# Keys, receptance and output projection of a recurrent block in three reduced-precision passes, and half of the values ahead of the triangular matrices

## The reference

```
h = rms_norm(x, norm_g)
dx = jnp.pad(h, ((0, 0), (1, 0), (0, 0)))[:, :-1] - h
xr, xw, xk, xv, xa, xg = (h + dx * mu[i] for i in range(6))
r = xr @ w_r
...
k = xk @ w_k
v = xv @ w_v
...
o = wkv7_scan(rh, decay, kh, vh, -kk, kk * ah)
...
y = (o + bonus.reshape(Bn, Sn, Dn)) * g.astype(f32)
return y.astype(x.dtype) @ w_o, v_first
```

## Time and profile before

| | us |
|---|---|
| median of 3 runs | 976.53 (975.99 to 976.78) |
| the profiled execution | 981.15 |
| its span | 979.4 |
| PE busy | 955.4 (98%) |
| DVE busy | 668.4 (68%) |
| ACT busy | 442.1 (45%) |
| one middle group, from second-rank matmuls to second-rank matmuls (91.47 to 156.51) | 65.04 |

### The profile page before, as it was taken

The page is one execution under the profiler, slowest core; times in us unless marked ns, Lnnn a source line. Parts: engine busy times, 40 slices in busy tenths (PEclk is TensorE's granted clock), DMA queues, the critical chain, the costliest instruction groups (busy, mean ns, idle before and its releaser), DMA issues.

```text
span 979.4 us, 17605 instructions
## 1 busy us (share of the span) xinstructions
PE 955.4 (98%) x6716; PEld 826.2 (84%) x6716; DVE 668.4 (68%) x1269; ACT 442.1 (45%) x708; POOL 84.5 (9%) x66
## 2 busy tenths in 40 slices
PE   8999999999999999999998999999999999999998
PEld 6778688686788888888897999999999798888887
DVE  7863755647647666666696878888887666666665
ACT  3313214114225444444355566666656554444442
POOL 0211000000010000000021222121212000000000
PEclk9999999999989999999998999999999999999999
DMA  9310320500513766666468455445543147666661
GB/s 303 135 57 1 115 72 1 172 14 4 171 43 99 224 192 193 188 189 194 115 215 240 116 157 154 131 128 162 148 143 116 46 131 221 190 190 188 185 188 59
DMA packets 195126, 136.85 MB, mean 140 GB/s; under 512 B 7278, under 2 KB 185966, under 8 KB 194940
## 3 DMA queue, kind: packets, MB, share of 16 engines
q1 hardware_dynamic: 195068, 136.03, 47.2%
HBM read 134.96 MB, written 1.05 MB: 139 GB/s over the span
## 4 chain that ended last, share of the span: by engine, by line
PE 63%; issue 24%; DVE 6%; POOL 4%; ACT 2%; POOLq 0%; DVEq 0%
PE wide L446 34%; PE bank L446 28%; POOL gsm L1834 4%; DVE work L1309 2%; DVE work L1312 1%; ACT work L994 1%; DVE x L1309 1%; DVE wsp L1309 0%; ACT L994 0%; DVE work L1567 0%; PE bank L469 0%; DVE am L1309 0%; DVE work L1399 0%; POOL small L1834 0%; DVE work L1619 0%
## 5 line engine op out<-in xcount | busy, mean ns | idle before, releaser
L446 PE MATMUL bank<-wpj,hkq 128*128 128x384 f32 x1152 | 216.9, 342 | 2.6 <-ACT Vs L994 1.8
L446 PEld LDWEIGHTS bank<-wpj,hkq 128*128 128x128 f32 x1152 | 199.9, 190 | 6.6 <-ACT wpj L994 2.8
L446 PE MATMUL wide<-hsp,wsp 128*128 128x256 f32 (+2 forms) x1120 | 193.4, 329 | 0.0
L446 PEld LDWEIGHTS wide<-hsp,wsp 128*128 128x128 f32 x1120 | 172.4, 190 | 23.0 <-DVE hsp L1309 0.6
L1309 DVE TENSOR_TENSOR wsp<-ring,wsp 128x1024 fp32r<-128x1024 f32 (+1 forms) x88 | 150.7, 1752 | 4.2 <-ACT wsp L994 4.2
L994 ACT ACTIVATE wsp<-ring 128x1024 fp32r<-128x1024 f32 (+1 forms) x88 | 130.3, 1485 | 21.9 <-PE wide L446 13.3
L1309 DVE TENSOR_TENSOR wpj<-ring,wpj 128x1536 fp32r<-128x1536 f32 x48 | 84.2, 1754 | 23.0 <-ACT wpj L994 23.0
L446 PE MATMUL bank<-wsp,asp 128*128 128x512 f32 x396 | 98.1, 392 | 0.0
L1834 POOL TENSOR_TENSOR gsm<-gsm,mhalf 128x6 f32<-128x6 f32 (+1 forms) x40 | 62.4, 1593 | 312.8 <-DVE gsm L1757 215.1
L446 PEld LDWEIGHTS bank<-wsp,asp 128*128 128x128 f32 x396 | 71.7, 189 | 13.1
L994 ACT ACTIVATE wpj<-ring 128x1536 fp32r<-128x1536 f32 x48 | 71.2, 1484 | 24.3 <-PE bank L446 16.6
(11 more groups left out here) (243 smaller groups left out, 1136.9 us busy)
## 6 DMA issues: line engine op xcount, KB each, us to landing
ring<-in_f_w_gu SPq DMA_DIRECT2D x88, 512.0 KB, 5.9
ring<-in_w_kv SPq DMA_DIRECT2D x96, 256.0 KB, 3.5
ring<-in_f_w_down SPq DMA_DIRECT2D x44, 512.0 KB, 3.7
ring<-in_b_w_q SPq DMA_DIRECT2D x48, 256.0 KB, 3.5
wmix<-in_a_w_k SPq DMA_DIRECT2D x4, 1024.0 KB, 7.8
wmix<-in_a_w_r SPq DMA_DIRECT2D x4, 1024.0 KB, 10.0
wmix<-in_a_w_v SPq DMA_DIRECT2D x4, 1024.0 KB, 5.2
wmix<-in_a_w_o SPq DMA_DIRECT2D x4, 1024.0 KB, 5.6
```

Of the source, the lines that this page charges most:

```text
L446: return pe.matmul(o, a, b, start=start, stop=stop)
```

## The change

Three projections of groups 1 to 3 go to the three-pass form: receptance (`project_parts` on `rw_hi`, `xr_hi`, `xr_lo`), keys, and the output product inside the loop (`product_o` for `it < NGRP`). Group 0's receptance and keys, the values, and the output product behind the last group stay float32. New copies: ACT writes `x_hi` (two tensors of 2048 columns, in group 0), `kw_hi`, `rw_hi`, `ow_hi` (2048 columns, in groups 0 to 2, for the group after) and `y_hi` (512 columns, in groups 1 to 3). DVE writes the low parts, in pieces of 1024 columns.

Four further moves: the value quarter that stood behind the second matrices now stands ahead of `turn_norms` (groups 1 to 3); the four scans of DVE run while POOL takes the root (`norm_output(it, 1, scans)`); a one-element sigmoid at a group's end brings the sigmoid table in ahead of the square; and several tiles share memory to make room. On SP the feed-forward loads wait once more, for the last receptance.

```
@@ DVE, in the levels and behind them
+                    if not behind and l in (1, 2):
+                        dve.wait_ge(S("act_x_hi"), 1)
+                        dve.wait_ge(S("pe_k"), 1)
+                        low_half("xk", l - 1)
+                    kw = l - (1 if behind else 3)
+                    if ahead and kw in (0, 1):
+                        low_key_weights(kw)
...
+                if not behind:
+                    dve.wait_ge(S("act_x_hi"), 2)
+                    dve.wait_ge(S("pe_r"), 1)
+                    low_half("xr", 0)
+                    low_half("xr", 1)
+                if ahead:
+                    low_query_weights()
+                if ahead and behind:
+                    low_output_weights()
                 dve.wait_ge(S("pe_S"), it + 1)
...
-                norm_output(it + 1, 0)
+                norm_output(it + 1, 0, None if behind else low_output_weights)
@@ ACT, behind the copies of the matrices and at the group's end
+                if ahead:
+                    act.wait_ge(s_wm[1], it * 16 + 32)
+                    A(kw_hi, wmix[:, 1, :], ACT.Copy).then_inc(S("act_mix_hi"), 1)
                 act.wait_ge(S("pe_v"), it + 1)
                 A(vT, bank[6], ACT.Copy).then_inc(S("act_v"), 1)
...
                 if ahead:
+                    A(small[:, 63:64], onec[:, 0:1], ACT.Sigmoid)
                     square_output(it + 1, 0)
@@ PE
+            def project_parts(b, i, hi, parts, name, quarters=range(4)):
+
+                w_parts = [v.rearrange("p (k n) -> p k n", k=KT) for v in (hi, mix_lo[:, i, :])]
+                for n, k0 in ((v // 2, v % 2 * (KT // 2)) for v in quarters):
+                    for k in range(k0, k0 + KT // 2):
+                        for a, c in PASSES:
+                            m = mm(bank[b][:, n * T:(n + 1) * T], w_parts[a][:, k, n * P:(n + 1) * P], parts[c][:, k, :],
+                                   k == 0 and a + c == 0, k == KT - 1 and a == 1)
...
-                project(6, 2, xv, "pe_v", range(early - 1))
+                project(6, 2, xv, "pe_v", range(early if behind else early - 1))
...
-                if behind:
-                    project(6, 2, xv, "pe_v", [early - 1])
@@ SP
+            sp.wait_ge(S("pe_r"), NGRP)
             ffn(0)
```

More of the change, by code:

```diff
@@ L107, in program @@
         raws.close()
+        x_hi = raws.enter_context(nc.sbuf_tensor("x_hi", [P, 3, KT * 256], F32R))
+        raws.close()
         sb("ring_head", [P, 5120])
@@ L112, in program @@
         wmix_low = sb("wmix_low", [P, KT, D], F32R)
-        WORK = 28000
+        WORK = 24588
         pg = sb("pg", [P, 2, NR + 1])
@@ L118, in program @@
         gsm = sb("gsm", [P, 64])
+        raws.enter_context(nc.sbuf_tensor("under_x_lo", [P, 2 * KT * T], F32))
+        x_lo = raws.enter_context(nc.sbuf_tensor("x_lo", [P, 2, KT * T], F32R))
+        raws.close()
         first = ExitStack()
         work = first.enter_context(nc.sbuf_tensor("work", [P, WORK], F32))
+        w_hi = first.enter_context(nc.sbuf_tensor("w_hi", [P, 2, KT * 256], F32R))
+        y_hi, y_lo = (first.enter_context(nc.sbuf_tensor(n, [P, 2, T], F32R)) for n in ("y_hi", "y_lo"))
         def C(name):
@@ L190, in program @@
         kT_ = cg.take(512, "p (n t) -> p n t", n=2)
-        rkr = cg.take(512, "p (n t) -> p n t", n=2)
+        rkr = t1
         bb = sq.rearrange("p n t -> p (n t)")
@@ L197, in program @@
         bv = nrm
-        Vn = cg.take(512, "p (c n i) -> p c n i", c=2, n=2)
-        kPn = cg.take(256, "p (n i) -> p n i", n=2)
-        bPn = cg.take(256, "p (n i) -> p n i", n=2)
+        spare_G, spare_E = (v.rearrange("p q t -> p (q t)")[:, 0:512] for v in (Gc, E1))
+        Vn = spare_G.rearrange("p (c n i) -> p c n i", c=2, n=2)
+        kPn, bPn = (spare_E[:, 256 * i:256 * i + 256].rearrange("p (n i) -> p n i", n=2) for i in range(2))
         Zs = cg.take(256)
-        UUs = cg.take(512, "p (c n i) -> p c n i", c=2, n=2)
+        UUs = sa.rearrange("p n t -> p (n t)").rearrange("p (c n i) -> p c n i", c=2, n=2)
         St = cg.take(256, "p (n i) -> p n i", n=2)
@@ L213, in program @@
         NGRP = D // 256
+        xr_hi, xk_hi = (x_hi[:, i, :].rearrange("p (k t) -> p k t", k=KT) for i in range(2))
+        xr_lo, xk_lo = (x_lo[:, i, :].rearrange("p (k t) -> p k t", k=KT) for i in range(2))
+        mix_lo = wmix_low[:, :, :].rearrange("p a d -> p (a d)").rearrange("p (i n) -> p i n", i=4)
+        rw_hi, kw_hi, ow_hi = x_hi[:, 2, :], w_hi[:, 0, :], w_hi[:, 1, :]
+        HALVES = (slice(0, KT * T // 2), slice(KT * T // 2, KT * T))
         WO_BANKS, WO_LAST = (0, 1, 7, 0), (0, 1, 5, 7)
@@ L536, in product_o @@
             def product_o(it, tiles=range(RT), done=0, halves_=range(2)):
-                pe.wait_ge(S("dve_y"), it + done)
-                if tiles[0] == 0:
-                    pe.wait_ge(s_wm[3], it * 16)
+                if it < NGRP:
+                    pe.wait_ge(S("dve_mix_lo"), it * 6)
+                    pe.wait_ge(S("dve_y_lo"), it)
+                else:
+                    pe.wait_ge(S("dve_y"), it + done)
+                    if tiles[0] == 0:
+                        pe.wait_ge(s_wm[3], it * 16)
                 for r in tiles:
@@ L1088, in group @@
                   ACT.Copy).then_inc(S("act_rn"), 1)
+                if behind:
+                    act.wait_ge(S("dve_y"), it)
+                    if it > 1:
+                        act.wait_ge(S("pe_wo"), it * 4 - 4)
+                    A(y_hi[:, :, :], yT[:, :, :], ACT.Copy).then_inc(S("act_y_hi"), 1)
                 if not behind:
@@ L1101, in group @@
                 A(bPn.rearrange("p n i -> p (n i)"), bank[4][:, 256:512], ACT.Copy).then_inc(S("act_kn"), 1)
+                if ahead:
+                    act.wait_ge(s_wm[0], it * 16 + 32)
+                    A(rw_hi, wmix[:, 0, :], ACT.Copy).then_inc(S("act_mix_hi"), 1)
+                if ahead:
+                    act.wait_ge(s_wm[3], it * 16 + 16)
+                    if it > 0:
+                        act.wait_ge(S("pe_wo"), it * 4)
+                    A(ow_hi, wmix[:, 3, :], ACT.Copy).then_inc(S("act_mix_hi"), 1)
                 if not ahead:
@@ L1488, in group, with scans, low_half, low_key_weights @@
                 two = bass.ds(it * 2, 2)
+                def scans():
+                    dve.wait_ge(S("act_sz"), it + 1)
+                    for n in range(2):
+                        for c in range(2):
+                            m = dve.tensor_tensor_scan(Gs[:, 2 * n + c, 1:129], onec[:, :], sz[:, n, c * P:(c + 1) * P], 0.0, ALU.mult, ALU.add)
+                    q.mark(m)
+                def low_half(kind, h):
+                    dst, raw_, hi = {"xk": (x_lo[:, 1, :], xk.rearrange("p k t -> p (k t)"), x_hi[:, 1, :]),
+                                     "xr": (x_lo[:, 0, :], xr.rearrange("p k t -> p (k t)"), x_hi[:, 0, :]),
+                                     "kw": (mix_lo[:, 1, :], wmix[:, 1, :], kw_hi), "rw": (mix_lo[:, 0, :], wmix[:, 0, :], rw_hi),
+                                     "ow": (mix_lo[:, 3, :], wmix[:, 3, :], ow_hi)}[kind]
+                    cut = HALVES[h]
+                    low_part(dst[:, cut], raw_[:, cut], hi[:, cut], "dve_x_lo" if kind[0] == "x" else "dve_mix_lo")
+                def low_key_weights(h):
+                    dve.wait_ge(S("act_mix_hi"), it * 3 + 1)
+                    low_half("kw", h)
+                def low_query_weights():
+                    dve.wait_ge(S("act_mix_hi"), it * 3 + 2)
+                    low_half("rw", 0)
+                    low_half("rw", 1)
+                def low_output_weights():
+                    dve.wait_ge(S("act_mix_hi"), it * 3 + 3)
+                    low_half("ow", 0)
+                    low_half("ow", 1)
                 if behind:
                     group_columns(it)
-                    norm_output(it, 1)
+                    norm_output(it, 1, scans)
+                else:
+                    scans()
                 dve.wait_ge(S("dve_pg"), it + 1)
[L1494 to L1498, removed]
+                q.sync()
                 step(tt(Gc[:, :, :], Gs[:, :, :], Gs[:, :, 64:65].broadcast_to([P, 4, 129]), ALU.subtract))
```

32 lines of the change are left out of this document (25 added, 7 removed).

## The result

| | before | after |
|---|---|---|
| median | 976.62 us (8 runs, 974.99 to 978.96) | 984.43 us (8 runs, 979.67 to 984.99) |
| ratio after/before | | 1.006, 95% interval 1.0042 to 1.0078 |
| profiled execution: time, span | 981.15, 979.4 us | 984.35, 982.6 us |
| its mean granted clock | 0.993 | 0.984 |

The change makes the kernel slower by 0.6%. The forecast was 974.3 us with a range up to 982.5: the sign is wrong and the time lies outside the range. It is the case that the prediction called rival one, new waits that cost clock, 0.4 us above the 980 to 984 that it gave for two to four of them.

The account below looks back on a forecast made before the run. TensorE looked like the bound, with DVE and ACT limiting some stretches; of a 10.8 us ceiling, added conversions and waits left -2.2 us: 978.95 against the profile, 974.3 us on the median, range 970 to 982.5.

Parts of the forecast that it names:

- rival one: New PE waits in group 0's levels, level 2 and seams cost clock: one fall 977.3, two to four 980-984; chances 0.20, 0.25.
- What bounds the kernel: Time mix: PE, DVE and ACT limit different stretches; three passes save 3.6 us of PE time a group, 10.8 in all.
- The rate of the passes: In the three-pass projections, float32r matmuls of 256 columns come every 0.12 us, so a quarter of twelve takes 1.44 us.
- sums to level 1: From the sums of squares to the first level of a group, the new kernel gains 2.05 us.
- Group 0's levels: Two low parts of the key weights behind levels 3 and 4 add 2.4 us on the path.
- The state's cover: Behind the levels, PE's output matmuls cover a state some 0.5 us late: zero cost; without cover 0.5 a group.
- The wait for the keys: Level 2 of groups 1 and 2: DVE waits for load and copy, PE behind it, 2.0 us each.
- The seam: Between groups: keys' 1.0 us lost, PE waits about 1.4 us, sums at -1.25; first seam's low parts add 1.25.
- the first case: The forecast's own sum for the whole kernel, -2.2 us, giving 974.3 us, range 971.5 to 977; chance 0.42.
- The base: Whole kernel: the -2.2 us, summed against the profiled 981.15, was put on the median, 4.6 us below it.
- Rival two: The keys' wait in level 2 of groups 1 and 2 is absent and 4.0 us come back: 970.3 us; chance 0.13.

Follow-up runs that it names:

- k_early: The changed kernel with the next group's key-weight load issued ahead of the output weights' load; 972.48 us, ratio 0.9944.
- kf_scans_back: kf_oe_fill with the four scans behind the normalised output again, as in the kernel before; 968.51 us, ratio 0.9921.
- ke_fill: k_early plus identity products ahead of the turned output (6, 3 and 3 at the seams) and 3 in group 3's wait; 969.35 us, ratio 0.9911.
- keys_fp32: The changed kernel with the key projection back in float32, without the copy and low parts of key weights or xk's low parts; 971.24 us, ratio 0.9941.
- out_only: keys_fp32 with the receptance projection in float32 too, leaving only the output product in three passes; 974.85 us, ratio 0.9962.
- before_wait: The kernel before plus unread DVE differences behind level 1 of groups 1 and 2 (3 and 4), injecting a wait; 985.72 us, ratio 1.0083.
- kf_out_early: keys_fp32 with group 0's low parts of the output weights moved from the seam to behind levels 1 and 2; 969.99 us, ratio 0.9926.
- before_wait_fill: before_wait with 6 and 10 identity products ahead of level 2's second products in groups 1 and 2; 982.83 us, ratio 1.0068.
- kf_oe_fill: kf_out_early plus three identity products ahead of the turned output at each seam and three in group 3's wait; 968.59 us, ratio 0.9905.

## Why the prediction was wrong, point by point

**What bounds the kernel** was read rightly: where PE is kept fed and at full clock, a middle group goes from 65.05 to 61.25 us, 3.8 where 3.6 of PE work was computed. That it fits is in part two errors against each other: half an output product went from 3.53 to 2.96 us and not to 2.75, and a key quarter from 1.93 to 1.61, 0.32 saved and not 0.25. **The rate of the passes** was right: in the new kernel successive three-pass matmuls start at 75.74, 75.86 and 75.98, 0.12 us apart. So was **sums to level 1**: -2.05 predicted, -2.08 to -2.10 measured. The matrices start when both inputs are there: in group 2 DVE's last product ends at 176.87 and PE starts them at 176.94, with no wait in the profile.

```profile
75.74 0.28 PE L459 MATMUL bank<-x_lo,w_hi 128*128 128x256 f32 x1
75.86 0.28 PE L459 MATMUL bank<-x_hi,wmix_low 128*128 128x256 f32 x1
75.98 0.28 PE L459 MATMUL bank<-x_hi,w_hi 128*128 128x256 f32 x1
```

**Group 0's levels** were mis-sized a little, +2.4 against +2.0 at level 5's first mask (70.31 before, 72.18 after, less a start that was 0.14 earlier): a low part takes 1.18 there and overlaps its neighbours. **The state's cover** of zero cost held: in group 0 the reduction behind it waited 0.72 us for PE, so the state held up nobody, and from level 2 of group 1 to the next sums k_early gains 1.71 us (+1.78 to +0.07) with the low parts in between.

**The wait for the keys** was right in mechanism, place and releaser, and its size was off in group 2: 3.20 instead of 2.0. The chain of work that ended last shows both loads, start and us to landing:

```profile
117.69 7.56 DMA wmix<-in_a_w_k
182.36 8.96 DMA wmix<-in_a_w_k
```

Level 1's second mask stands 4.67 us behind the issue in both groups (122.36 and 187.03), where the prediction's sum had 4.73. So what differs between 1.82 and 3.20 us is the landing: 7.6 and 9.0 us, the second just outside the 6.8 to 8.8 of the range. Why group 2's took longer is open.

**The seam** failed in its working. I took the keys' 1.0 us for lost and PE's wait, 1.4 us by my sum, for the scans' doing; it is 0.96, kf_scans_back shows no such price, and from level 2 to the next sums ke_fill gains 1.71 a group where 1.25 was forecast. At the seam of groups 0 and 1 the sum had 1.4 and 1.25, a wait of 2.65 us, and the profile has 2.00. POOL's root takes 1.91 us there beside DVE's low parts instead of 1.02, which costs nothing more: it ends at 93.27, the low parts at 93.54, and DVE's product starts at 93.46. The term that was missing is the fall behind the wait, 6.8 us at half clock.

**The step that failed** is the choice between the first case and rival one. The forecast's sum had no clock in it. The prediction had seen that a wait of 0.92 us is followed by the lower level and gave new falls together 0.45, yet took "no fall" as the likeliest single case, because the Trainium skill (TensorE: Matmul & The Clock Gate, HAM oscillation) warns only of idle gaps longer than any wait here, and because 0.82 us at the seams had no fall behind it. The measurement decides: falls come with waits of 1.68 (keys_fp32), 1.87, 2.00, 2.96 and 3.26 us among work that is not dense, and not with those of 0.96, 1.08 (out_only), 1.33, 1.70 (before_wait) and, behind seven products, 1.60. The length alone doesn't decide it: group 3's wait is 0.92 us in each of the nine profiles where it is not filled, and six of them have a fall within some 2.5 us behind it, three (keys_fp32, kf_out_early, before_wait_fill) have none. What else decides is open. Three new falls, at the first seam and in level 2 of groups 1 and 2, bring the prediction's own price, 980 to 984 us: put in front of the same waits, the products bring 975.23, 0.9 above the forecast. It also took half of group 3's fall, 3.2 us (3.4 by shorter stretches), as the price of one; the one of group 2 lasts 10.2 us at half and costs 4.0 on the path.

**The base.** I added the displacement to the median on the footing that the profiled execution's surplus of 4.6 us is common to both kernels. It was two falls, group 3's and the one at 522 us, that come together in a third of the executions. Profile against profile the new kernel is 3.2 us longer, median against median 7.8.

**Rival two** (the wait absent, 970.3) is what k_early and ke_fill build, and they measure 972.48 and 969.35: the sum without clock and without the keys' wait came within 1 us of ke_fill, where the clock stays up. That is in part luck: at group 3's level 1 that sum stands at -6.25 and ke_fill at -8.64, for the seams and group 0 gave 2.4 us more than I counted, and the median shows 1 of it. What the keys' passes themselves bring is small for another reason: they save 0.92 us in each of the two later groups, but group 0 pays 2.0 us for them and for the output weights' low parts at the seam, against kf_oe_fill.

## What to carry to other kernels

Price a new wait of the matrix engine twice: with its own length, and with the stretch at half clock that may follow; if the trace shows one such fall anywhere, give it a good chance at every new wait of that size among small matmuls. When a conversion is put between a load and its user, look at what the load stands behind in its queue before counting flops: here the order of two loads turned a gain of 0.6% into a loss of 0.6%. Compare clocks of several executions before adding a displacement to one of them.

## What the runs showed of the hardware

- A short wait costs more than itself: 2.96 us of injected wait put 7.55 us between the masks of levels 2 and 3 instead of 4.40. Products of the identity in the wait (0.13 us a record) kept the granted clock at 1.00 in every place where they were tried in the time mix, even where 1.6 us of waiting were left behind them.
- The falls are not the same in each execution: the kernel before has mean clocks from 0.993 to 0.999 and times from 981.1 down to 973.5 us with them. The same wait of 0.92 us is followed by a fall in six profiles and by none in three.
- A root of 4 columns on POOL takes 1.02 us, and 1.91 when DVE computes a low part, two inputs from SBUF, at its side. By the Trainium skill (GPSIMD Engine Reference, Key points) POOL shares its SBUF interfaces with DVE, and contends with DVE instructions that read two SBUF inputs; the trace agrees.
